# ScalarE copies a bank out before it converts the next weights: order of ScalarE's work in five stages, and TensorE's order in step 10

## What is computed

```python
# first block: two attention branches of 8 heads, gated and merged
h = rmsnorm(x, norm_g) * (1 + scale) + shift            # scale, shift, gate from c @ w_ada
q_a, k_a, v_a, z_a, q_b, k_b, v_b, z_b, f, g = split(h @ w_in)
y_a = (stick_breaking(q_a, k_a, v_a) * silu(z_a)) @ w_o_sb
y_b = (forgetting_attention(q_b, k_b, v_b, f) * silu(z_b)) @ w_o_fox
g1, g2 = sigmoid(g + b_gate)
x = rmsnorm(x + gate * ((g1 * y_a + g2 * y_b) @ w_out), final_g)
# second block: differential attention beside a causal convolution
q, k, v, u = split(rmsnorm(x) @ w_in_2)                 # 4 heads x 2 maps, q and k rotated
a = rmsnorm((softmax(q1 k1) - lam * softmax(q2 k2)) @ v)
c = silu(layernorm(conv31(u[:512] * sigmoid(u[512:])) + b))
x = x + concat(a, c) @ w_out_2
x = x + cross_attention(rmsnorm(x), rmsnorm(mem))       # 256 memory rows, K and V from w_ckv
x = x + conv_ffn(rmsnorm(x));  return rmsnorm(x)
```

## Time and profile before

| | us |
|---|---|
| median of 3 runs | 1373.19 (1373.02 to 1374.03) |
| the profiled execution, its own time | 1374.46 |
| its span, first to last instruction | 1372.7 |
| busy: PE, PEld | 1305.2, 1081.6 |
| busy: DVE, POOL, ACT | 761.0, 734.3, 569.1 |
| mean granted TensorE clock | 0.977 of 2.4 GHz |

### The profile page before, as it was taken

The page is one execution under the profiler, slowest core; times in us unless marked ns, Lnnn a source line. Parts: engine busy times, 40 slices in busy tenths (PEclk is TensorE's granted clock), DMA queues, the critical chain, the costliest instruction groups (busy, mean ns, idle before and its releaser), DMA issues.

```text
span 1372.7 us, 17264 instructions
## 1 busy us (share of the span) xinstructions
PE 1305.2 (95%) x6330; PEld 1081.6 (79%) x6330; DVE 761.0 (55%) x1302; ACT 569.1 (41%) x919; POOL 734.3 (53%) x858
## 2 busy tenths in 40 slices
PE   5999999989999899999989999999999999999997
PEld 5778788868788778787767897887878888888875
DVE  5756777433334247698677525774537715651653
ACT  2555465544455336322444555343433413331331
POOL 0733443432333476576342687632739967875772
PEclk9989999999999999999998899999999999999998
DMA  9621224222323642222213344320322333333221
GB/s 333 211 77 47 78 69 146 78 92 70 122 87 115 221 135 85 84 91 94 77 57 113 99 133 140 107 74 19 108 77 92 107 108 93 92 107 93 93 77 61
DMA packets 41700, 142.81 MB, mean 104 GB/s; under 512 B 4624, under 2 KB 5008, under 8 KB 40464
## 3 DMA queue, kind: packets, MB, share of 16 engines
q1 hardware_dynamic: 41616, 141.71, 32.0%
HBM read 131.21 MB, written 8.39 MB: 102 GB/s over the span
## 4 chain that ended last, share of the span: by engine, by line
PE 77%; DVE 14%; ACT 5%; DMA 2%; issue 2%; POOL 1%; DVEq 0%; SPq 0%; ACTq 0%; POOLq 0%
PE ps L135 76%; DVE tm L145 3%; DVE ac L148 3%; DMA raw<-units 2%; ACT tm L142 1%; PE ps L139 1%; ACT wh L142 1%; DVE x L148 1%; ACT L142 1%; DVE tm L148 1%; DVE spl L145 1%; DVE ma L148 0%; DVE sph L156 0%; POOL ycl L145 0%; ACT hh L142 0%
## 5 line engine op out<-in xcount | busy, mean ns | idle before, releaser
L145 POOL TENSOR_TENSOR wl<-raw,wh 128x256 fp32r<-128x256 f32 x804 | 679.8, 878 | 579.2 <-ACT wh L142 579.1
L142 ACT ACTIVATE wh<-raw 128x1024 fp32r<-128x1024 f32 x201 | 212.5, 1057 | 452.9 <-PE ps L135 443.5
L135 PE MATMUL ps<-hh,wh 128*128 128x512 f32 x872 | 345.2, 396 | 2.8 <-DVE cb L145 1.6
L135 PE MATMUL ps<-hh,wl 128*128 128x512 f32 x872 | 341.2, 391 | 0.0
L135 PE MATMUL ps<-hl,wh 128*128 128x512 f32 x872 | 341.2, 391 | 0.0
L135 PEld LDWEIGHTS ps<-hh,wh 128*128 128x128 f32 x872 | 164.8, 189 | 37.7 <-DVE cb L145 1.8
L135 PEld LDWEIGHTS ps<-hh,wl 128*128 128x128 f32 x872 | 164.7, 189 | 35.2
L135 PEld LDWEIGHTS ps<-hl,wh 128*128 128x128 f32 x872 | 165.0, 189 | 33.1
L148 DVE SCALAR_TENSOR_TENSOR tm<-cb,par_sb,tm 128x512 f32<-128x512 f32 x88 | 87.1, 990 | 50.5 <-ACT tm L142 47.1
L145 DVE TENSOR_TENSOR tm<-tm,tm 128x512 f32<-128x512 f32 (+3 forms) x106 | 91.6, 868 | 39.6 <-ACT tm L142 36.8
L142 ACT ACTIVATE tm<-tm 128x512 f32<-128x512 f32 (+3 forms) x109 | 54.2, 531 | 95.2 <-DVE tm L148 79.2
(11 more groups left out here) (309 smaller groups left out, 2366.8 us busy)
## 6 DMA issues: line engine op xcount, KB each, us to landing
raw<-units SPq DMA_DIRECT2D x217, 512.0 KB, 3.5
kept<-ge SPq DMA_DIRECT2D x16, 256.0 KB, 2.0
tm<-kept SPq DMA_DIRECT2D x16, 256.0 KB, 3.7
tm<-gate_w SPq DMA_DIRECT2D x12, 256.0 KB, 4.1
x<-xin SPq DMA_DIRECT2D x2, 1024.0 KB, 9.8
x<-xin SPq DMA_DIRECT2D x1, 2048.0 KB, 10.1
out<-x SPq DMA_DIRECT2D x8, 256.0 KB, 2.2
kv<-kvt SPq DMA_DIRECT2D x1, 1536.0 KB, 8.5
```

Of the source, the lines that this page charges most:

```text
L135: return self.none if self.e is None else self.e.matmul(out, lhs, rhs, start=start, stop=stop, skip_group_check=skip)
L142: return self.none if self.e is None else self.e.activation(out, in_, func, **kw)
L145: return self.none if self.e is None else self.e.tensor_tensor(out, a, b, op)
```

## The change

In `qk_high`, `z_gate`, `gate` and `dproj` ACT first reads the bank and then calls `refill` of the same unit. In `conv` the bias copy of bank 1 comes first, too. In the 16 steps, at odd n the refill of a convolution unit goes behind `turn_d(n)`; from step 10 on the refill for `kv(p, 0)` goes behind `turn_d(n)` as well. The last bias copy, for x = 15, which PE's step 10 completes, is issued by ACT at the end of step 9, ahead of `join_d(10)`, and step 10 keeps only the refill, now behind `pv_d(4)`. On PE, step 10 does `turn_d(10)` ahead of `kv(0, 0)`. No instruction is added or taken away, and VectorE's, GpSimd's and SyncE's programs stay as they are.

```diff
--- before.py
+++ after.py
@@ -1030,7 +1030,7 @@
                     qk_d(n + 2)
                 if step is not None:
                     dproj(h, step)
-                if n >= KV_STEP:
+                if n > KV_STEP:
                     kv(n - KV_STEP, 0)
             else:
                 if step is not None:
@@ -1045,6 +1045,8 @@
             turn_d(n)
             if step in (1, 4):
                 dproj(h, step + 1)
+            if n == KV_STEP:
+                kv(0, 0)
             if n >= KV_STEP:
                 kv(n - KV_STEP, 1)
             if n == 11:
@@ -1298,29 +1300,29 @@
 
         def qk_high(br, c, what):
             p = c % 2
-            refill((br + what, c))
             act.wait_ge(s_unit, (br + what, c))
             if before_q(br, c):
                 act.wait_ge(s_z, *before_q(br, c))
             d, s = {"q": (Qh, s_qh), "k": (Kh, s_kh)}[what]
             act.fn(d[p][:, :], PS[qkz_bank(br, c, what)][:, :], ACT.Copy).then_inc(*s.up(br, c))
+            refill((br + what, c))
 
         def z_gate(br, c):
-            refill((br + "z", c))
             act.wait_ge(s_unit, (br + "z", c))
             if br == "a" and c < 2:
                 act.wait_ge(s_hl, "1", 7)
             else:
                 act.wait_ge(s_yl, *before_z(br, c))
             act.fn(SZ[c % 2][:, :], PS[qkz_bank(br, c, "z")][:, :], ACT.Silu).then_inc(*s_sz.up(br, c))
+            refill((br + "z", c))
 
         def gate(n):
-            refill(gate_unit(n))
             act.wait_ge(s_unit, gate_unit(n))
             if n >= 3:
                 act.wait_ge(l_kept[n % 3], n - 3)
             act.fn(GE[n % 3][:, :], PS[1 - n % 2][:, :], ACT.Identity,
                    bias=pcol("b_gate", gate_unit(n)[1])).then_inc(*s_gl.up(n))
+            refill(gate_unit(n))
 
 
         def qk_a(h):
@@ -1475,11 +1477,14 @@
         vproj("d", "dv", V2h)
 
         def conv(x):
-            j, q = 2 + x // 8, x // 2 % 4
-            if x % 2 == 0:
-                return
-            refill(("cw", j, q))
-            if q == 3:
+            conv_out(x)
+            if x % 2:
+                refill(("cw", 2 + x // 8, x // 2 % 4))
+
+        def conv_out(x):
+
+            j = 2 + x // 8
+            if x % 8 == 7:
                 act.wait_ge(s_unit, ("cw", j, 3))
                 act.fn(AC[j][:, :], PS[1][:, :], ACT.Identity, bias=pcol("cv_dw_b_2", j)).then_inc(*s_ac.up(j))
 
@@ -1490,12 +1495,12 @@
             b, nm = 0, ("dq", "dk")[step // 3]
             if step % 3 != 1:
                 return
-            refill((nm, h))
             act.wait_ge(s_unit, (nm, h))
             n = d_order.index((nm, h))
             if n:
                 act.wait_ge(s_rot, *d_order[n - 1])
             act.fn(RTh[:, :], PS[b][:, :], ACT.Copy).then_inc(*s_rh.up(nm, h))
+            refill((nm, h))
 
         def qk_d(n):
             m = 128 * (n % 4 + 1)
@@ -1555,23 +1560,31 @@
         join_d(0)
         for n in range(16):
             h, step = d_step(n)
-            if n and n % 2 == 0 and n != KV_STEP:
+            convs = range(cw_done(n), cw_done(n + 1))
+            if n and n % 2 == 0:
                 pv_d(n // 2 - 1)
             if n % 2 == 0:
-                for x in range(cw_done(n), cw_done(n + 1)):
-                    conv(x)
-            if n == KV_STEP:
-                pv_d(n // 2 - 1)
+                for x in convs:
+                    if n == KV_STEP:
+                        refill(("cw", 3, 3))
+                    else:
+                        conv(x)
             if step is not None:
                 dproj(h, step)
             if n < 14:
                 qk_d(n + 2)
             if n % 2:
-                for x in range(cw_done(n), cw_done(n + 1)):
-                    conv(x)
+                for x in convs:
+                    conv_out(x)
+            turn_d(n)
+            if n % 2:
+                for x in convs:
+                    if x % 2:
+                        refill(("cw", 2 + x // 8, x // 2 % 4))
             if n >= KV_STEP:
                 refill(kv_units(n - KV_STEP)[0])
-            turn_d(n)
+            if n == KV_STEP - 1:
+                conv_out(15)
             if n < 15:
                 join_d(n + 1)
             if n >= KV_STEP:
```

## The result

| | before | after |
|---|---|---|
| median of 4 runs each, us | 1373.61 (1373.02 to 1374.18) | 1356.46 (1356.13 to 1357.11) |
| ratio | | 0.9876, 95% interval 0.9863 to 0.9888 |
| profiled execution: span, us | 1372.7 | 1355.3 |
| mean granted clock | 0.977 | 0.983 |

The change returns 17.15 us; 11.5 had been forecast. The direction was right, and the time lies on the low edge of the range, 1356.5 (the four runs went from 1356.13 to 1357.11); so the question is where another 5.6 us came from.

A forecast was written before the change was run, and what follows sets the result against it. TensorE, busy 95% of the span, was taken as the bound, with ordering able to recover its waits. Terms 2.6 + 1.5 + 0.97 + 1.9 + 0.96 + 3.2 + 0.4 = 11.5 us gave 1361.7 us, range 1356.5 to 1368.5.

The forecast's parts named there:

- Gates: Gate units: PE's three waits for ScalarE's copy into `ge` return 0.8 + 0.8 + 0.96 = 2.6 us.
- Rotations, convolution, odd steps: Second block's steps, 644 to 719 us: earlier rotation copies, bias copy and turns return 1.5, 0.97 and 1.9 us.
- The two microseconds that were to stay at `dkl`: Step 5, PE's wait ending at 718.81: about 2 us of the 2.47 us wait for VectorE's `dkl` remain.
- Steps 9 and 10: Step 9's rotation chain returns 0.96 us; step 10's earlier bank copy and turn inside the former wait return 2.2 us.
- The clock at `kv(0, 0)`: First memory value unit: less PE idling ahead may avoid its half clock, 0 to 2.1 us, taken as 1.0.
- I take the middle: Clock term at `kv(0, 0)`: 1.0 us chosen between 0 if the clock falls and 2.1 if it holds.
- q, k and z: First block's projections: earlier `kh` would still wait for VectorE's `ewl`, so the 1.83 us `kl` wait returns 0.
- The bound above, 0.96: Projections q, k, z: at most 0.96 us gained if VectorE could have run `kl`'s chain first.
- VectorE beside GpSimd: First branch's steps: the later `wl` subtraction shifts against VectorE's split chain; 0.4 us, bounds -1.0 to +1.0.
- the clock holds, and more often: Rival: no fall after 753 and one or two further half-clock falls spared; 15 us gain, 1358 us, chance 0.15.
- `ac` gone: Sign of being right: PE's waits for ScalarE's copies into `ac` gone or under 0.3 us.
- `kl` near 166 unchanged: Sign of being right: PE's wait for `kl` in the first block, 1.83 us, stays as before.

The follow-up runs named there:

- e1: The kernel before with ScalarE's bank copy moved ahead of the refill in `gate` alone; 1373.7 us, ratio 1.0003 to before.
- e2: The kernel before with ScalarE's copy ahead of the refill in `qk_high`, `z_gate` and `gate`, steps as before; 1365.32 us, ratio 0.9940.
- e12: The kernel after with `gate` alone put back to refill first; 1358.06 us, ratio 0.9886 to before.
- e4: The kernel before with GpSimd's subtraction waiting for ScalarE's copy of q, k, z and gate banks, ScalarE's order unchanged; 1369.42 us, ratio 0.9960.
- e10: The kernel before with ScalarE's swap in `gate` alone plus GpSimd's subtraction waiting for ScalarE's bank copies; 1367.89 us, ratio 0.9958.
- e5: The kernel after with PE's old order at step 10, `kv(0, 0)` ahead of `turn_d(10)`; 1355.71 us, ratio 0.9853 to before.
- e3: The kernel after with `qk_high`, `z_gate` and `gate` put back to refill first, leaving the steps' edits; 1362.2 us, ratio 0.9913 to before.
- e7: The kernel before with 11 matmuls that nothing reads added in front of `kv(0, 0)`; 1371.7 us, ratio 0.9971.
- e13: The kernel after, unedited, timed again like the experiments; 1356.25 us, ratio 0.9866 to before.

## Why the prediction was right, and where it wasn't

**Gates: 2.6 forecast, 2.7 found** (E in after, e1, e2; undone in e12). The step is right.

**Rotations, convolution, odd steps: 1.5 + 0.97 + 1.9 forecast for 644 to 719 us; 3.9 found in G,** and 0.3 just ahead of it. Right, within what G scatters (3.3 to 3.9, since it is 74.0 in e1, e4 and e10). The two microseconds that were to stay at `dkl` stayed: 1.79.

**Steps 9 and 10: 0.96 + 2.2 forecast; idle time fell by 1.6.** The waits gave half of the term; that the stretch as a whole returned more than forecast is luck. The waits for `tm` and `ac` went as described. But PE came sooner by 2.7 us of full clock in H, and VectorE's chain didn't, so the `dkl` wait grew by 1.0. H is 4.3 us shorter, 2.7 of it for a reason that the sum did not have there. The swap of PE's order was credited with filling the old wait; by e5 it is worth nothing that can be measured.

**The clock at `kv(0, 0)`: 1.0 forecast.** There the clock still fell, for a shorter part (0.67 against 0.55 over 5.2 us; the 24 matmuls of the unit took 4.44 us instead of 5.02), and then near 768 for 6.8 us, where before had 3.4. I is 0.7 us longer than before. With the same code in the steps, e3 and e12 have 35.1, 2.7 shorter than before. So the step "I take the middle" was no estimate: the term is between -0.7 and 2.7. e7 shows that the mechanism was right for the long wait; behind the pieces that are left of it (0.33, 1.59 and 0.51 us) a half clock came again.

**q, k and z: 0 forecast. This is the step that failed,** though the time fell on the edge of the range. The prediction read `ewl` as a fixed 1.09 us that blocks `kl`, and concluded that an earlier `kh` would wait for VectorE. The 1.09 was no property of `ewl`: it was 0.69 plus a wait for GpSimd's subtraction, and the change moves that subtraction. The bound above, 0.96, was for ScalarE's copy alone and so was no bound. B returned 2.4 us (the waits at 160.02 and for `kl`). In A, idle time fell by 1.6: PE's waits at 92.79, 94.80 and 159.29 for `spl` and `sph` were 0.56, 0.75 and 0.59 and are 0.15, 0.22 and none. C's 1.5 is a half-clock stretch at 170.7 of before; it can't be put down to the `kl` wait ahead of it, since e1 has that wait and no such stretch, and e10 has the stretch behind a wait of 0.63. The prediction was right in one thing here: an earlier `kh` alone would have waited for VectorE. `kl` starts at the end of `ewl` in before, after, e4 and e10 alike.

**VectorE beside GpSimd: 0.4 forecast, bounds -1 to +1.** The prediction named the right mechanism for `sph` and `spl` and sized it as if each instruction stood alone. They stand in one chain with `ewl` and `kl`, and what each loses adds up (24.46 us against 22.52). e4, which moves GpSimd and nothing else, is worth 4.9 us (interval 3.4 to 7.4).
The Trainium skill (SBUF — State Buffer, Who interferes with whom) says more than the prediction took from it: casts can contend as well as instructions with two SBUF inputs, and there the one that issues first has the shared ports for the whole instruction while the other "fully blocks"; issue order decides which one that is. The trace agrees that order decides: `sph`, a cast, 0.78 us behind GpSimd's start against 0.36 ahead of it; `ewl` 1.09 when it starts 0.22 us behind GpSimd, 0.69 when it starts 0.16 ahead.

**The sum.** Of the 17.4 us between the two profiles, PE's busy time fell by 6.4; that is mostly the clock, net of places where it fell anew. The other 11 us are idle time. Of them 7.1 are in the terms of the sum (E 2.2, G 3.3, H 1.6) and 3.7 in VectorE's chain (A 1.6, B 2.1); the rest nearly cancels. The prediction had 10.1 for the waits (with 0.16 us of record for each), 1.0 for the clock and 0.4 for VectorE beside GpSimd. The waits came to 1 to 2 us less than forecast, VectorE's chain and the clock to more. The rival "the clock holds, and more often" (1358 us) came nearest in time, in part by luck: it had nothing for VectorE's chain, the fall at `kv(0, 0)` that it struck out did come, and no stretch behind the gates was spared. What it had right is H, where none came.

**What was to show it.** Right: `ac` gone, `ge` down to the remainder of one wait, 0.8 us (not gone: 1.72 less 0.96 was always 0.76), the turn's wait of 0.51, no wait for weights, a mean clock above before's. Wrong: "`kl` near 166 unchanged".

What stays open: why single half-clock stretches differ between executions of the same code (D is 117.7 or 120.5 us), how much of the 6.4 us is due to which edit, and so the exact sum of e2 and e3.

## What to carry to other kernels

Where an engine both empties banks and prefetches for later, let it empty first; then look at who starts next behind the prefetch, since a third engine's work moves too. Before taking a duration as fixed, compare it with the shortest of the same form in the tile's row: 1.09 against 0.69 is a wait in disguise, and it can be won without touching the instruction. And judge single waits by the time between the same two matmuls rather than by the total, as 2.7 us of return can vanish under one or two half-clock stretches (e1).

## What was not expected of the hardware

- An instruction's length depended on less than 0.4 us of order: `ewl` took 0.69 us where it began just ahead of GpSimd's subtraction (e4) and 1.09 just behind it (before). The other side pays too: those four subtractions took 3.17 us in e4, and four like them 2.79 in another place (464.27 of after).
- Adding 11 matmuls (2.8 us of them) to a wait made the kernel 3.1 us faster (e7).
- The half-clock stretches of after came again at the same places in a second profile (e13), and yet they are not fixed by the code: e5, with the same code until 735 us, has others, and e3, whose first 600 us have the code of before, had 6.8 us at half clock near 97 where before had 10.2.
